# More block products in the down projection of eight feed-forward stages

## The reference, cut to what matters

```python
D_MODEL = 1024
D_FF = 2816

def swiglu(h, w1, w3, w2):
    return (jax.nn.silu(h @ w1) * (h @ w3)) @ w2
...
        h = rmsnorm(x, g_ffn1[l])
        x = x + 0.5 * swiglu(h, w1_a[l], w3_a[l], w2_a[l])
```

## Time and profile before

| | |
|---|---|
| median of 3 runs | 2238.62 us (2238.1 to 2239.01) |
| the profiled execution | 2236.88 us |
| its span (first to last instruction) | 2235.1 us |
| PE matmul busy | 2228.8 us, 100% |
| PE weight load busy | 1902.8 us, 85% |
| DVE busy | 1754.6 us, 79% |
| ACT busy | 1292.0 us, 58% |
| POOL busy | 0.2 us |
| granted TensorE clock | 1.00 of full |
| DMA | 417.64 MB, mean 187 GB/s |

### The profile page before, as it was taken

One profiled execution on the slowest core, in us unless ns is written; L12 is line 12 of the kernel. 1 busy time (PEld: TensorE's weight loads), 2 busy tenths in 40 slices (PEclk: granted clock), 3 DMA queues, 4 the chain that ended last, 5 costly groups with the idle time before them and its releaser, 6 DMA issues.

```text
span 2235.1 us, 29208 instructions
## 1 busy us (share of the span) xinstructions
PE 2228.8 (100%) x11590; PEld 1902.8 (85%) x11590; DVE 1754.6 (79%) x2451; ACT 1292.0 (58%) x1545; POOL 0.2 (0%) x4
## 2 busy tenths in 40 slices
PE   9999999999999999999999999999999999999999
PEld 8888888888888888888888888888888888788887
DVE  7886567888788566788888799767888887976787
ACT  6655445565664544655655576565555647755663
POOL 0000000000000000000000000000000000000000
PEclk9999999999999999999999999999999999999999
DMA  7656555654565555574565553546555645355562
GB/s 266 226 180 217 166 188 182 228 197 149 201 216 171 176 171 206 170 244 142 198 222 183 190 171 127 199 163 226 179 179 202 205 156 196 105 167 195 199 216 99
DMA packets 176217, 417.64 MB, mean 187 GB/s; under 512 B 16816, under 2 KB 20784, under 8 KB 176080
## 3 DMA queue, kind: packets, MB, share of 16 engines
q1 hardware_dynamic: 175936, 415.76, 55.0%
q10 hardware_dynamic: 144, 0.00, 0.0%
HBM read 414.66 MB, written 1.05 MB: 186 GB/s over the span
## 4 chain that ended last, share of the span: by engine, by line
PE 93%; DVE 4%; ACT 3%; issue 1%; DMA 0%; SPq 0%; DVEq 0%; ACTq 0%
PE psum L737 25%; PE psum L673 14%; PE psum L675 14%; PE psum L674 14%; PE psum L738 13%; PE psum L867 2%; PE psum L866 2%; PE psum L864 2%; PE psum L705 2%; ACT split_w L1290 2%; DVE split_w L1788 1%; PE psum L748 1%; PE psum L1090 1%; DVE split_w L1795 0%; DVE gate L1937 0%
## 5 line engine op out<-in xcount | busy, mean ns | idle before, releaser
L1788 DVE TENSOR_TENSOR split_w<-raw,split_w 128x2048 fp32r<-128x2048 f32 (+2 forms) x373 | 807.6, 2173 | 130.5 <-ACT split_w L1290 128.7
L737 PE MATMUL psum<-xt,split_w 128*128 128x512 f32 x2464 | 859.0, 393 | 0.5 <-DVE split_w L1788 0.5
L1290 ACT ACTIVATE split_w<-raw 128x2048 fp32r<-128x2048 f32 (+2 forms) x373 | 674.9, 1821 | 128.1 <-PE psum L675 91.1
L738 PE MATMUL psum<-xt,split_w 128*128 128x256 f32 x2464 | 689.2, 280 | 0.0
L737 PEld LDWEIGHTS psum<-xt,split_w 128*128 128x128 f32 x2464 | 461.2, 187 | 104.7 <-DVE split_w L1788 2.2
L738 PEld LDWEIGHTS psum<-xt,split_w 128*128 128x128 f32 x2464 | 465.3, 189 | 0.3
L673 PE MATMUL psum<-split_w,xt 128*128 128x512 f32 (+1 forms) x736 | 289.5, 393 | 0.0
L675 PE MATMUL psum<-split_w,xt 128*128 128x512 f32 (+1 forms) x736 | 283.7, 385 | 0.0
L674 PE MATMUL psum<-split_w,xt 128*128 128x512 f32 (+1 forms) x736 | 283.6, 385 | 0.0
L673 PE MATMUL psum<-split_w,ht_hi 128*128 128x512 f32 x444 | 173.5, 391 | 0.2 <-DVE split_w L1788 0.2
L675 PE MATMUL psum<-split_w,ht_lo 128*128 128x512 f32 x444 | 172.9, 390 | 0.0
(11 more groups left out here) (306 smaller groups left out, 2772.3 us busy)
## 6 DMA issues: line engine op xcount, KB each, us to landing
raw<-w_in_dram SPq DMA_DIRECT2D x180, 512.0 KB, 4.5
raw<-t_gate_up_1b_dram SPq DMA_DIRECT2D x88, 512.0 KB, 4.4
raw<-t_gate_up_2a_dram SPq DMA_DIRECT2D x88, 512.0 KB, 4.5
raw<-t_gate_up_2b_dram SPq DMA_DIRECT2D x88, 512.0 KB, 4.7
raw<-t_gate_up_1a_dram SPq DMA_DIRECT2D x84, 512.0 KB, 4.6
raw<-ffn_w_down_dram SPq DMA_DIRECT2D x48, 512.0 KB, 4.4
raw<-w_a_dram SPq DMA_DIRECT2D x24, 512.0 KB, 4.5
raw<-w_b_dram SPq DMA_DIRECT2D x24, 512.0 KB, 4.6
```

What stands on the lines that cost most here:

```text
L737: nc.tensor.matmul(bank, whi[:, slot, w], xt[:, c, :, :], start=c == 0, stop=False)
L738: last = nc.tensor.matmul(bank[:, 0:T], wlo[:, slot, w], xt_hi[:, c, :], start=False, stop=c == DC - 1)
L1290: nc.scalar.activation(whi[:, e.unit(u) % HL, 0:n], raw[:, r, 0:n], ACT.Copy).then_inc(hi_done, 1)
L1788: nc.vector.tensor_tensor(wlo[:, e.unit(u) % HL, 0:n], raw[:, r, 0:n], whi[:, e.unit(u) % HL, 0:n], ALU.subtract).then_inc(w_ready, 1)
```

## The change

It is made to the feed-forward stages alone.

- Six pairs of chunks (2 to 13) in two groups (`SUPER`) of three, in place of four pairs; 10 chunks remain alone. A quarter of a group is a unit of 1536 columns. Each product of the seven is two units of 9 matmuls.
- Quarters 11, 22 and 21 are ring units of their own, and the sums are built in `early_sums` and `late_sums`: U = 11 (loaded by SP) with 12 added by an accumulating DMA that POOL issues; T2 = U + 22 on DVE, with 22 read from its ring slot; T3 = 12 (loaded by SP) + 22 on DVE in the same way; T4 = T2 + 21 by an accumulating DMA. Quarters 11, 12 and 21 are thus read from memory twice.
- The order of units is plain, U, 11, plain, 22, T2, 21, plain, T3, T4 (each product twice, once a group), then the three plain units of the second column half. It was plain, plain, 11, 21, plain, U, 22, plain, T2, plain, T4, T3, plain, plain, plain.
- Gate/up: one DVE instruction adds gate and up of a block, and scaling, silu, hidden and its splits run once for two blocks; the sums of hidden halves run in six of eleven pairs of blocks, in three instructions.
- The down weights are laid out on the host so that each unit is one contiguous run a partition.

The diff, cut to its core:

```diff
-MIXED = range(4, 20, 4)
-ALONE = ((0, 1, 2, 3), (6, 7, 10, 11), (14, 15, 18, 19), (20, 21))
-DOWN = (("plain", 0, ALONE[0]), ("plain", 0, ALONE[1]), ("product", "11"), ("product", "21"),
-        ("plain", 0, ALONE[2]), ("product", "U"), ("product", "22"), ("plain", 1, ALONE[0]),
-        ("product", "T2"), ("plain", 0, ALONE[3]), ("product", "T4"), ("product", "T3"),
-        ("plain", 1, ALONE[1]), ("plain", 1, ALONE[2]), ("plain", 1, ALONE[3]))
+SUPER, PAIRS = 2, 3
+QUARTER = 512 * PAIRS
+MIXED = range(1, 1 + SUPER * PAIRS)
+ALONE = ((0, 1, 14, 15), (16, 17, 18, 19), (20, 21))
+DOWN = ((("plain", 0, 0),) + each("sum", "U") + each("quarter", "11") + (("plain", 0, 1),) + each("quarter", "22")
+        + each("sum", "T2") + each("quarter", "21") + (("plain", 0, 2),) + each("sum", "T3") + each("sum", "T4")
+        + tuple(("plain", 1, i) for i in range(3)))
+BY_VECTOR = ('T2', 'T3')
...
# SP, ffn_loads
+                    if b in (12, 14):
+                        s = (b - 12) // 2
+                        eng.wait_ge(ht_done, ffn_pairs(e, f, 1))
+                        sum_load(early_sums, "11", s, w2, early_in)
                 for i, part in enumerate(DOWN):
-                    if i == 12:
+                    if i == AT["quarter", "22", 0]:
                         eng.wait_ge(w_used, units(e, u0 + 2 * FG - 1, HL))
-                        quarter_load(w2, "12")
-                        quarter_load(w2, "22")
+                        for s in range(SUPER):
+                            sum_load(late_sums, "12", s, w2, late_in)
...
# POOL, new
+            def accumulate(q, s, w2):
+                eng.dma_start(early_sums[:, s, :], quarter(e, w2, q, s), accum_op=ALU.add).then_inc(added_in[s], 16)
+
+            def down_sums(u0, f, w2):
+
+                for s in range(SUPER):
+                    eng.wait_ge(early_in[s], 32 * (ffns(e, f) + 1))
+                    accumulate("12", s, w2)
+                for name, before in (("T2", "U"), ("T4", "T2")):
+                    for s in range(SUPER):
+                        if name in ACCUMULATE:
+                            if before in ACCUMULATE:
+                                eng.wait_ge(added_in[s], accumulated(e, f, ACCUMULATE.index(before) + 1))
+                            eng.wait_ge(w_ready, units(e, u0 + 2 * FG + AT["sum", before, s], RAW))
+                            accumulate(ADDED[name], s, w2)
...
# DVE
+            def sum_added(u, f, name, s):
+
+                eng.wait_ge(raw_in[e.place(u) % RAW], loaded(e, u))
+                if name == "T3":
+                    eng.wait_ge(late_in[s], 32 * (ffns(e, f) + 1))
+                out = sum_tile(name, s)
+                nc.vector.tensor_tensor(out, out, raw[:, e.place(u) % RAW, 0:QUARTER], ALU.add).then_inc(combined, 1)
...
+                for i in range(1, FG):
+                    block_summed(2 * i)
...
+                    block_summed(2 * i + 1)
+                    gate_scaled(i)
...
+                    hidden(i)
+                    if i in MIXED:
+                        sums(i)
+                    hidden_lo(i)
+                    if i in MIXED:
+                        sums_lo(i)
...
+                splits("quarter", "11")
+                down_split(at("plain", 0, 1))
+                used(at("quarter", "11"))
                 part_to_x(0, 0, EACH, rhalf).then_inc(taken, 1)
...
                 for m in range(MT):
                     part_to_x(m, 1, BOTH, rhalf)
...
+                for s in range(SUPER):
+                    sum_added(u0 + 2 * FG + at("quarter", "22", s), f, "T2", s)
+                    sum_added(u0 + 2 * FG + at("quarter", "22", s), f, "T3", s)
+                    down_split(at("quarter", "22", s))
+                splits("sum", "T2")
+                splits("quarter", "21")
+                down_split(at("plain", 0, 2))
+                used(at("sum", "T2"))
+                split_before(at("plain", 0, 2))
                 part_to_x(0, 1, EACH, minus_half).then_inc(taken, 1)
...
+                splits("sum", "T3")
+                splits("sum", "T4")
+                used(at("sum", "T3"))
+                split_before(at("sum", "T4"))
+                part_to_x(1, 0, EACH, rhalf)
+                part_to_x(1, 1, EACH, minus_half)
+                used(at("plain", 0, 2))
+                part_to_x(0, 0, psum[:, 4, :], rhalf)
+                down_split(at("plain", 1, 0))
+                split_before(at("plain", 1, 0))
+                used(at("sum", "T4"))
+                last = part_to_x(1, 0, psum[:, 5, :], rhalf)
...
# PE
+                alone(0, 0, True, False)
                 eng.wait_ge(pair_free, ffn_blocks(e, f, FC - 1))
...
+                products("U")
+                products("11")
+                eng.wait_ge(ht_done, ffn_pairs(e, f, 9))
+                alone(0, 1, False, False)
+                products("22")
                 eng.wait_ge(taken, 2 * ffns(e, f) + 1)
...
+                products("T2")
+                products("21")
+                eng.wait_ge(ht_done, ffn_pairs(e, f, 10))
+                alone(0, 2, False, (True, False))
                 eng.wait_ge(taken, 2 * ffns(e, f) + 2)
...
+                products("T3")
+                products("T4")
```

More of the change, by code:

```diff
@@ L446, in mix_tables, with sum_tile, by_vector, quarter @@
             return 16 * (per[1] * min(e.layer() + 1, LAYERS) + per[2] * max(e.layer() + 1 - LAYERS, 0))
+        def sum_tile(name, s):
+            return late_sums[:, s, :] if name == "T3" else early_sums[:, s, :]
+        def by_vector(e, f, name, s):
+            n = len(BY_VECTOR) * SUPER
+            return n * (2 * e.layer() + f) + len(BY_VECTOR) * s + BY_VECTOR.index(name) + 1
+        def quarter(e, w2, q, s):
+            return a[w2 + "_quarters"][rows_of((e.lay * SUPER * 4 + s * 4 + QUARTERS.index(q)) * P, P), :]
+        def plain_rows(e, w2, half, i):
+            first = sum(len(chunks) for chunks in ALONE[:i])
+            return a[w2 + "_alone"][rows_of((2 * e.lay + half) * P, P), 512 * first:512 * (first + len(ALONE[i]))]
         block = ctx.enter_context(nc.Block())
@@ L492, in wide, with sum_load @@
                     plain(w, D, 4 * P * k, col, u + k, 4, cols)
-            def quarter_load(w2, q):
-                first = e.lay * FF + P * MIXED.start
-                rows = w2[first:first + 4 * P * len(MIXED), :].rearrange("(k four p) n -> p k four n", four=4, p=P)
-                row, col = int(q[0]) - 1, int(q[1]) - 1
+            def sum_load(out, q, s, w2, semaphore):
+                half = QUARTER // 2
                 for j in range(2):
-                    eng.dma_start(quarter[q][:, 1024 * j:1024 * j + 1024].rearrange("p (k n) -> p k n", k=2),
-                                  rows[:, 2 * j:2 * j + 2, row, 512 * col:512 * col + 512]
-                                  ).then_inc(quarter_in[q], 16)
@@ L504, in alone, with down_load @@
-            def alone(w2, chunks, col, u):
-                k = len(chunks) // 2
-                rows = [e.lay * FF + P * chunks[j * k] for j in range(2)]
-                load(u, [(chunked(512 * j * k, k, 512),
-                          w2[rows[j]:rows[j] + k * P, col:col + 512].rearrange("(k p) n -> p k n", p=P))
+                    cols = slice(j * half, j * half + half)
+                    eng.dma_start(out[:, s, cols], quarter(e, w2, q, s)[:, cols]).then_inc(semaphore[s], 16)
+            def down_load(u, part, w2):
+                if part[0] == "plain":
+                    _, half, i = part
+                    n, rows = 512 * len(ALONE[i]), plain_rows(e, w2, half, i)
+                else:
+                    n, rows = QUARTER, quarter(e, w2, part[1], part[2])
+                load(u, [(chunked(j * n // 2, 1, n // 2), rows[:, j * n // 2:(j + 1) * n // 2].unsqueeze(1))
@@ L871, in ffn_tensor @@
-                u = u0 + 2 * FG
+                    for s in range(SUPER):
+                        u = u0 + 2 * FG + AT["quarter" if name in QUARTERS else "sum", name, s]
+                        slot = e.unit(u) % HL
+                        eng.wait_ge(w_ready, units(e, u, RAW))
+                        for k in range(PAIRS):
+                            hi, lo = LEFT[name](MIXED.start + s * PAIRS + k)
+                            w = slice(k * 512, (k + 1) * 512)
+                            final = stop and s == SUPER - 1 and k == PAIRS - 1
+                            nc.tensor.matmul(out, hi, whi[:, slot, w], start=start and s == 0 and k == 0, stop=False,
+                                             skip_group_check=resumed)
+                            nc.tensor.matmul(out, hi, wlo[:, slot, w], start=False, stop=False,
+                                             skip_group_check=resumed)
+                            last = nc.tensor.matmul(out, lo, whi[:, slot, w], start=False, stop=final,
+                                                    skip_group_check=resumed)
+                        last.then_inc(w_used, 1)
@@ L1360, in ffn_scalar @@
```

(7 more changed lines are left out.)

356 lines of the change are left out of this document (157 added, 199 removed).

## The result

The changed kernel takes **2281.21 us** (median of 4 runs, 2278.51 to 2286.8) against 2238.36 before, measured beside it on the same chip: a ratio of 1.0195, 95% interval 1.0172 to 1.0218. It is 1.95% slower. The forecast was 2272, so the sign and four fifths of the size came out; some 9 us are missing from it.

A forecast was written before the change was run, and what follows sets the result against it. PE, busy 100%, was taken to bound the kernel. New waits of 45.8 us, less 10.9 for matmuls and 1.3 for old waits, gave +33.6, so 2272 against the 2238.62 median; forecast 2263 to 2280 (50%), wider range 2248 to 2320.

The forecast's parts named there:

- 48 matmuls removed: On PE, six fewer matmuls in each of eight down stages at 0.2267 us each: 10.9 us (0.5%) saved.
- Gate/up in twos: In gate/up, DVE work for a pair of blocks (9.1 us of 11.0) fits under PE's matmuls: zero in both directions.
- the three waits of before: PE waits in the first down stage of the old kernel, 1.3 us, taken off as replaced by the new waits.
- The chain on DVE, first and second wait: Down stage: 7.0 us of DVE work behind product 11 makes PE wait 2.00, then 2.85 us, before the 22 units.
- The third wait: PE waits 0.55 us a stage, plus 0.11, for the first unit of the other column half, split late by DVE.
- rival (a): Accumulating DMAs late, T4's split waits: PE waits 5 to 9 us more a stage, 2312 to 2344; chance 27%.
- Transfers hidden: Down-stage loads of 22, 12 and U and T4's accumulating DMA land in time, zero cost; queue share 55% to 60%.
- The value taken, 8: Assumed landing time in us of T4's accumulating DMA, with 12 us allowed, so zero cost.
- The estimate of 3.8 us: Skill page's 2.0 us plus bytes at 436 GB/s: one 786 KB sum by GpSimd-issued DMA takes 3.8 us, costing nothing.
- "Collectives: The Full Stack": Page saying adds inside a transfer need two source reads and halve the rate; by it the accumulating DMAs would be late.
- (b): Down stage: DVE not late, only the matmuls count, if sums cost half a split; 2226 to 2228; chance 14%.
- (c): Down stage: the DVE chain makes PE wait, but less than forecast, 2245 to 2263; chance 9%.

## Why the prediction came out as it did, step by step

**48 matmuls removed, 10.9 us: right.** The page counts 48 fewer, and with them at 0.2267 all but 0.8 of 52.3 us has its place.

**Gate/up in twos, zero: right as a sum.** Tried alone, 0.9994 (0.9985 to 1.0003). Behind it are a loss of 1.9 us ahead of the first down stage and a gain of 2.0 in it. So the three waits of before went by this part of the change, and were not "replaced by the new ones"; the forecast took them off for a wrong reason.

**The chain on DVE, first and second wait: right, to 0.12 us.** The price of 1536 columns, taken halfway between 1024 and 2048, is 1.67 measured from start to start (505.44, 507.11, 508.77). DVE goes on 13.85 after the stage's start (forecast 13.90), PE at 20.97 (21.04). The step can be trusted beyond the fit of the numbers, since removing the sums removed both waits, removing 1.32 us of DVE took 1.31 off the first, and doubling the sums took the list of these waits from 35.1 to 78.6 us.

**The third wait, 0.55 a stage: mis-sized as a sum, 6.8 against 4.4.** The chain gives 0.43, as the run without T4's sum shows. The rest, 3.3 us in four stages, is rival (a) in small.

**Transfers hidden: right but for those 3.3 us.** The load of 22 was forecast at 12.7 and ACT took it up at 11.9. POOL issued T4's accumulating DMAs at 27.9 and 29.7 after the stage's start (forecast 27.6 and 29.3), each issue keeping POOL for 0.87 us. The row that shows the lateness, of the stage from 489.6 on:

```profile
530.83 1.49 ACT L1337 ACTIVATE split_w<-early_sums 128x1536 fp32r<-128x1536 f32 x1 [3.14 <-DMA early_sums<-w_b_quarters_dram]
```

The issue at 519.36 and this start are 11.5 us apart. All DMAs into early_sums, issues (KB each, median us to landing) and the tile's landing times, of the changed kernel:

```profile
raw<-ffn_w_down_alone_dram SPq DMA_DIRECT2D x32, 512.0 KB, 7.1
early_sums<-ffn_w_down_quarters_dram POOLq DMA_DIRECT2D x16, 768.0 KB, 8.4
...
early_sums<-w_a_quarters_dram POOLq DMA_DIRECT2D x8, 768.0 KB, 8.0
early_sums<-w_b_quarters_dram POOLq DMA_DIRECT2D x8, 768.0 KB, 8.2
...
DMA to landing us min/median/max: 5.6/7.3/11.4
```

The value taken, 8, is the median of the accumulating ones. But T4's come in pairs: the first lands in 6.5 to 7.7 us, the second, issued 1.8 us behind it, in 9.8 to 11.4. In the first four stages the second has landed 40.6, 41.2, 40.7 and 40.4 us after the stage's start, and there the third wait is 0.74, 1.26, 0.80 and 0.48 above its 0.44. That is the time of landing less 39.9, to 0.04. The forecast would have allowed the second group 45.2 - 1.5 - 1.75 - 0.1 = 41.9, since it asked when PE takes T4. But in DVE's list three additions to x and the split of the next plain unit stand behind T4's split, and PE's third wait is for that unit. In the stage from 489.6 on DVE stood before T4's split and then had no rest:

```profile
532.35 1.76 DVE L1858 TENSOR_TENSOR split_w<-early_sums,split_w 128x1536 fp32r<-128x1536 f32 x1 [2.80 <-ACT split_w L1337]
```

So this step had the wrong deadline, by 2 us, and one landing time for two DMAs. In the last four stages the landings are at 39.6, 40.7, 39.9 and 41.2 and the third wait is 0.44; where they are latest, the half clock had held PE itself back by 1.6 us.

The three waits of before that were to go are 1.8 by starts, not 1.3: the list leaves out 0.16 each.

The estimate of 3.8 us by the Trainium skill, page "DMA: Bandwidth & Descriptors" (Anatomy of one DMA, SWDGE path), is not borne out for an accumulating DMA: the medians are 8.0 to 8.4, and none of the 32 landed in under 6.5. What "Collectives: The Full Stack" (The bandwidth ceiling) says of adds that need two source reads and halve the rate goes the same way as these medians; no run here isolates it, as other loads are under way beside them.

**Left out of the sum: TensorE's clock, 4.6 us in the profiled execution and more in others.** This is the step that failed by omission. The profile before shows a granted clock of 1.00 in every slice, with no wait of PE above 0.8 us once its work has begun, and so nothing that would have priced a fall. After, the fall comes at the second wait at L900, also where the first wait is only 0.57 (additions to x later: five stages), and in no down stage where the second is 1.16 or less (emptied sums, T2 by DMA).

**Left out as well: 1.6 us ahead of the first down stage.** In the first feed-forward stage PE waits for a split of ACT that waits 1.54 us for the load of a gate/up unit. Windows of both kernels there run at about all the DMA engines give (before, 0.98 of them busy; after, 1.03 from 8 to 24 us at 389 GB/s). The same wait is there with gate/up in twos alone (1.3 us), and not in the kernel before, so it belongs to that part of the change as far as one profiled execution of each can say. Over the other experiments it is 0.6 to 2.0 us, and with the sums emptied it is gone and another of 1.1 us stands at 9.97. Why the load is late was not tried.

Sum of the deviations in the profiled execution: -0.9 -0.2 +2.4 (waits) +4.6 (clock) +1.6 (start) -0.5 (waits of before) +0.8 (scattered) = +7.8; 2278.51 stands against 2270.5, +8.0, since the execution took 2.0 over its span and not 1.8. The median lies 2.7 higher again, and its runs go with the mean clock.

**The rivals.** (b) was turned down because the sums would have to cost half of a split; with the sums emptied its sign came true, 2232.5, though not its 2226 to 2228. (c) is out: the two waits are as long as forecast. (a) is there with 3.3 us of its 40 to 72.

## What to carry to other kernels

When PE is at 100%, count matmuls saved, and then walk the in-order engine that feeds it from each point where it must wait for PE: what it has to do from there to the next tile that PE takes, against the matmuls that PE still has in hand. Here 7.0 us of work stood against 5.4 us, and the waits cost 38 us where the 48 matmuls saved 10.9; the same products in another order, with the sums off that stretch, ran 0.2% faster than before. An operation ahead of such a split costs its full duration, wherever the engine's average busy share stands (1.32 us taken out gave 1.31). Ask the same of every transfer: its deadline is set by all that the in-order engine does behind it. And a wait of PE may cost more than its length, as the matmuls behind it may run at half the clock.

## What the hardware showed that I had not expected

- The granted clock falls to 1.2 GHz around waits of 2.7 us, with another of 1.7 or of only 0.4 us two microseconds before, and it fell once behind a single wait of 2.0 us (the other order, T2 by DMA). Two others of 2.0 us, among the third waits, passed without it. It stays there some 3 us and costs 1.3 to 1.6 us each time. With waits of 5.3 and 4.4 us it is down before each of them ends. Between equal stages of one execution it comes or stays away, and that makes the times of such a kernel spread: 2278.51 to 2286.8, against 2237.51 to 2239.01 before.
- It can fall with the engine at work again, up to 1.5 us behind the end of the wait.
- An accumulating DMA of 768 KB lands in 8.0 to 8.4 us (medians; 6.5 to 11.4; where two are issued 1.8 us apart the second takes 9.8 to 11.4), and the plain units of 512 KB that the ring loads beside them take 7.1 to 7.2 where those of before took 4.4 to 4.6, though the DMA engines' share over the whole span rose from 55% to 60% only. The plain units are also laid out otherwise than before, so no run isolates the cause.
